# HGRN mixer: half-column level masks, decoded outer products on TensorE, and the next stage's first slabs split one stage earlier

## The reference, cut to what matters

```python
def gla_chunked(q, k, v, log_f, s0):          # chunks of 64 tokens, 4 heads of 128
    ...
        b = jnp.cumsum(gc, axis=1)
        o_inter = jnp.einsum('bthk,bhkv->bthv', qc * jnp.exp(b), s)
        diff = b[:, :, None] - b[:, None, :]
        decay = jnp.where(causal, jnp.exp(jnp.minimum(diff, 0.0)), 0.0)
        att = jnp.einsum('bthk,bshk,btshk->bths', qc, kc, decay)
        o_intra = jnp.einsum('bths,bshv->bthv', att, vc)
        bl = b[:, -1]
        s_new = jnp.exp(bl)[..., None] * s + jnp.einsum('bshk,bshv->bhkv', kc * jnp.exp(bl[:, None] - b), vc)
```

## Time and profile before

| | before |
|---|---|
| median of 3 runs | 2322.16 us (2321.26 to 2322.62) |
| profiled execution, its own time | 2319.34 us |
| its span in the profile | 2317.6 us |
| PE busy | 2205.4 us (95%) |
| DVE busy | 1703.0 us (73%) |
| ACT busy | 1312.3 us (57%) |
| POOL busy | 1005.7 us (43%) |

### The profile page before, as it was taken

One profiled execution on the slowest core, in us unless ns is written; L12 is line 12 of the kernel. 1 busy time (PEld: TensorE's weight loads), 2 busy tenths in 40 slices (PEclk: granted clock), 3 DMA queues, 4 the chain that ended last, 5 costly groups with the idle time before them and its releaser, 6 DMA issues. The chain is left out here.

```text
span 2317.6 us, 46270 instructions
## 1 busy us (share of the span) xinstructions
PE 2205.4 (95%) x15487; PEld 1987.3 (86%) x15487; DVE 1703.0 (73%) x3914; ACT 1312.3 (57%) x3001; POOL 1005.7 (43%) x807
## 2 busy tenths in 40 slices
PE   8889899999999999999989898999999999999998
PEld 8878699999999877888878787999999997788886
DVE  6787379959999656666646555899699995566666
ACT  5434365557777555555546544645577765555554
POOL 6654246997777600000033243389877773000000
PEclk9989899999999999999989999999999999999999
DMA  7728454554444565555544483445444446555553
GB/s 268 126 77 332 185 174 148 170 179 149 155 156 155 199 206 173 185 189 184 187 137 152 144 355 126 164 163 171 163 155 157 154 150 218 191 189 184 189 186 123
DMA packets 115512, 409.33 MB, mean 177 GB/s; under 512 B 20026, under 2 KB 22242, under 8 KB 110050
## 3 DMA queue, kind: packets, MB, share of 16 engines
q1 hardware_dynamic: 111328, 391.45, 50.9%
q0 software_dynamic: 4032, 15.86, 2.1%
HBM read 397.11 MB, written 10.14 MB: 176 GB/s over the span
## 5 line engine op out<-in xcount | busy, mean ns | idle before, releaser
L2011 POOL TENSOR_TENSOR slab_ring_lo<-slab_ring,u_hi 128x512 fp32r<-128x512 f32 x512 | 676.9, 1347 | 182.9 <-ACT u_hi L2107 182.2
L2053 PE MATMUL banks<-operand_hi,u_hi 128*128 128x264 f32 x2048 | 595.7, 291 | 2.7 <-POOL slab_ring_lo L2011 2.7
L2055 PE MATMUL banks<-operand_hi,slab_ring_lo 128*128 128x264 f32 x2048 | 584.9, 286 | 0.0
L2054 PE MATMUL banks<-operand_lo,u_hi 128*128 128x264 f32 x2048 | 584.0, 285 | 0.0
L270 POOL TENSOR_TENSOR slab_ring_lo<-slab_ring,slab_hi 128x512 fp32r<-128x512 f32 x152 | 203.8, 1343 | 667.4 <-ACT slab_hi L260 661.5
L2463 DVE TENSOR_TENSOR operand_lo<-slab_ring,operand_hi 128x512 fp32r<-128x512 f32 x512 | 353.0, 692 | 130.6 <-ACT operand_hi L2428 126.3
L2511 PE MATMUL banks<-operand_hi,w_hi 128*128 128x512 f32 x1024 | 409.7, 400 | 9.9 <-DVE w_lo L2459 9.9
L2512 PE MATMUL banks<-operand_hi,w_lo 128*128 128x512 f32 x1024 | 407.7, 398 | 0.0
L2513 PE MATMUL banks<-operand_lo,w_hi 128*128 128x512 f32 x1024 | 407.6, 398 | 0.0
L2053 PEld LDWEIGHTS banks<-operand_hi,u_hi 128*128 128x128 f32 x2048 | 388.3, 190 | 4.6 <-POOL slab_ring_lo L2011 3.5
L2107 ACT ACTIVATE u_hi<-slab_ring 128x512 fp32r<-128x512 f32 x512 | 322.0, 631 | 122.0 <-PE banks L2055 121.3
(11 more groups left out here) (401 smaller groups left out, 3746.8 us busy)
## 6 DMA issues: line engine op xcount, KB each, us to landing
slab_ring<-in_u SPq DMA_DIRECT2D x256, 512.0 KB, 3.3
slab_ring<-in_v SPq DMA_DIRECT2D x256, 512.0 KB, 4.2
slab_ring<-in_proj SPq DMA_DIRECT2D x144, 512.0 KB, 3.4
cache_k_T<-in_cache_k SPq DMA_DIRECT2D x16, 1024.0 KB, 8.7
cache_v<-in_cache_v SPq DMA_DIRECT2D x16, 1024.0 KB, 13.1
memory_T<-in_mem POOLq DMA_DIRECT2D x2, 1024.0 KB, 5.1
sample_state<-in_state POOLq DMA_DIRECT2D x1, 2048.0 KB, 11.5
out_mem_k_out<-mem_k_T SPq DMA_DIRECT2D x16, 128.0 KB, 2.3
```

Source lines behind the costliest of these rows:

```text
L2011: nc.gpsimd.tensor_tensor(step.ring_lo[:, s, g * HC:(g + 1) * HC, :], step.slab(s)[:, g * HC:(g + 1) * HC, :], hi[:, buf].bitcast(F32), AL ...
L2053: nc.tensor.matmul(bank, hi[:, buf, k, :], xh[:, c, :], start=(c == 0), stop=False)
L2054: nc.tensor.matmul(bank, hi[:, buf, k, :], xl[:, c, :], start=False, stop=False)
L2055: last = nc.tensor.matmul(bank, step.ring_lo[:, s, c, :], xh[:, c, :], start=False, stop=(c == DC - 1))
```

## The change

The gates' iota in PSUM, which the change's name mentions, is in both versions. What differs:

1. `masked`: only the queries of the second run of each pair carry anything new at a level, so mask and add run on half of the 1024 columns, in runs of `half` (every second column at level 0). Level "0" (the identity mask) stays whole.
2. Decoded states: PE transposes the samples' values and keys to rows in `mixer_in` (two transposes after product 18); ACT copies them to SBUF; POOL makes blocks `value row x one-hot sample` on 32 partitions; `outer(k)` on PE multiplies the key rows by such a block, so that four outer products lie in a bank; DVE does `s0 = s0 * fg + bank` in one instruction for each of the four 128-column states. POOL's four decays (L1179) and DVE's L1253, L1258 go.
3. DVE's splits of slabs 6 to 12 move to POOL; POOL also splits slabs 16 and 17, the next block's first two, and ACT rounds them at the end of `mixer_attention`. In layer 1 the same two are split at the end of `window_prompt`. `Fold` with split=2 leaves them out.
4. `difference(2)` and `qe` move from the end of `mixer_in` to the start of `mixer_attention` on DVE, and PE waits for `qe` before the third product.
5. Memory pair 11 moves from before the outputs to after them, 12 from before the norm's means to after.
6. The pooling contexts are gathered by two ACT copies into one tile and stored after the second memory-key store instead of first.

```diff
@@ class Fold
-    def __init__(self, step, layer, which, count, room):
+    def __init__(self, step, layer, which, count, room, split=0):
...
-        split_high(step, act, self.base)
+        if not self.split:
+            split_high(step, act, self.base)
...
         for j in range(DC + self.count):
-            split_low(step, pool, self.base + j, (0,))
+            if j >= self.split:
+                split_low(step, pool, self.base + j, (0,))
...
-    fold = Fold(step, layer, 0, DC, room)
+    fold = Fold(step, layer, 0, DC, room, 2)
@@ mixer_in, PE
+                    if j == 18:
+                        pe.wait_ge(s_cp, H4)
+                        pe.wait_ge(s_kk, 1)
+                        pe.wait_ge(step.constants_ready, 32)
+                        for w, src in enumerate((vi, kk)):
+                            last = nc.tensor.transpose(ps[0:NS, 6, w * P:(w + 1) * P], src[:, NP:NP + NS], step.ident)
+                        last.then_inc(s_rT, 1)
@@ mixer_in, DVE
                     elif n == H4 + 2:
                         difference(dve, 1)
-                        difference(dve, 2)
-                        dve.wait_ge(s_eb, 1)
-                        nc.vector.tensor_tensor(qe[:], qs[:, 0:NP], ecum[:], ALU.mult)
@@ mixer_attention, SP
-                step.store(sp, io["pool_prompt"], u_ext[:, :, TP:TP + CTX])
-                step.store(sp, io["pool_sample"], s_ext[:, :, :, 1:CTX + 1])
                 for k in range(2 * DC):
+                    if k == 2:
+                        sp.wait_ge(s_po, 1)
+                        step.store(sp, io["pool_prompt"], pool_out[:, :, 0, :])
+                        step.store(sp, io["pool_sample"], pool_out[:, :, 1:, :])
@@ mixer_attention, PE
+                def outer(k):
+                    pe.wait_ge(s_row, 1)
+                    pe.wait_ge(s_dg, k // 4 + 1)
+                    if k:
+                        pe.wait_ge(s_kv, k)
+                    nc.tensor.matmul(ps[:, 6, :], rows[:, 1, :], blocks[k // 4][:, 512 * (k % 4):512 * (k % 4 + 1)],
                                      start=True, stop=True).then_inc(s_vb, 1)
...
-                memory_pair(5 + NL)
                 sample_out(6)
...
-                memory_pair(12)
+                memory_pair(11)
                 pool_product(2)
...
+                memory_pair(12)
+                pool_product(3)
                 memory_pair(13)
-                pool_product(3)
@@ mixer_attention, ACT
                 def high_and_copy(k):
-                    if k + 2 < 2 * DC:
-                        split_high(step, act, base + k + 2)
+                    split_high(step, act, base + k + 2)
@@ mixer_attention, POOL (the loop over windows)
                 for g in range(H4):
-                    low(8 + g, (0,))
+                    low(7 + g, (0, 1))
...
-                for k in range(13, 2 * DC):
+                for k in range(7 + H4, 2 * DC + 2):
                     low(k, (0, 1))
@@ mixer_attention, DVE
                 def masked(n, bank, mask):
                     dve.wait_ge(s_pd, n + 1)
...
+                    if n > 1:
+                        dve.wait_ge(s_ad, n - 1)
+                    half = CHUNK if n == 1 else LEVELS[n - 2]
...
+                    view = lambda ap: ap.rearrange("p (s n two t) -> p s n two t", s=NP // P, two=2, t=half)[:, :, :, 1, :]
+                    once = mask.rearrange("p (n two t) -> p n two t", two=2, t=half)[:, :, 1, :]
...
+                        nc.vector.tensor_tensor(view(part), view(two_banks(bank)),
+                                                once.unsqueeze(1).to_broadcast([P, NP // P, P // (2 * half), half]),
+                                                ALU.mult).then_inc(s_mk, 1)
+                    dve.wait_ge(s_mk, n + 1)
+                    nc.vector.tensor_tensor(later(att), later(att), later(part), ALU.add).then_inc(s_ad, 1)
...
                 def sample_state(k):
-                    dve.wait_ge(s_fs, k // 2 + 1)
+                    dve.wait_ge(state_ready, 16)
                     dve.wait_ge(s_vb, k + 1)
-                    outer = diag[k // 4][:, 512 * (k % 4):512 * (k % 4 + 1)].rearrange("p (a b) -> p a b", a=4)
-                    nc.vector.tensor_tensor(outer, ps[:, 6, :].rearrange("p (a b) -> p a b", a=4),
-                                            kk[:, NP + 4 * k:NP + 4 * k + 4].unsqueeze(2).to_broadcast([P, 4, P]),
-                                            ALU.mult).then_inc(s_kv, 1)
-                    dve.wait_ge(s_kv, 2 * k + 1)
-                    st = s0[:, 4 * k:4 * k + 4, :]
-                    nc.vector.tensor_tensor(st, st, outer, ALU.add).then_inc(s_kv, 1)
+                    for c in range(4 * k, 4 * k + 4):
+                        last = nc.vector.scalar_tensor_tensor(out=s0[:, c, :], in0=s0[:, c, :], scalar=fg[:, NP + c:NP + c + 1],
+                                                              in1=ps[:, 6, (c % 4) * P:(c % 4 + 1) * P], op0=ALU.mult, op1=ALU.add)
+                    last.then_inc(s_kv, 1)
...
                 operand(dve, 0)
+                difference(dve, 2)
+                nc.vector.tensor_tensor(qe[:], qs[:, 0:NP], ecum[:], ALU.mult).then_inc(s_qe, 1)
...
                 for i in range(NL):
-                    split_low(step, dve, base + 6 + i, (1,))
                     if i and i + 1 < NL:
                         operand(dve, i + 1)
```

More of the change, by code:

```diff
@@ L306 @@
 class Fold:
-    def __init__(self, step, layer, which, count, room):
-        self.step, self.layer, self.which, self.count = step, layer, which, count
+    def __init__(self, step, layer, which, count, room, split=0):
+        self.step, self.layer, self.which, self.count, self.split = step, layer, which, count, split
         self.base = step.used
@@ L440, in vector @@
                                     ALU.subtract).then_inc(self.mixed_lo, 1)
-            if c == HC - 1:
+            if c == HC - 1 and not self.split:
                 split_low(step, dve, self.base, (1,))
@@ L1435, in _ @@
                 pool.wait_ge(s_k, 1)
-                for k in range(2, 2 * DC):
+                for k in range(2, 2 * DC + 2):
                     split_low(step, pool, base + k, (0,))
-                slabs_split(step, pool, base + 2 * DC - 1)
+                slabs_split(step, pool, base + 2 * DC + 1)
             @block.sync
```

110 lines of the change are left out of this document (53 added, 57 removed).

## The result

| | before | after |
|---|---|---|
| runs beside each other, median | 2321.71 us (4 runs, 2318.59 to 2322.62) | 2298.75 us (4 runs, 2289.42 to 2302.72) |
| ratio, 95% interval | 1 | 0.9906 (0.989 to 0.9923) |
| the same kernel a second time | 2315.49 us (12 runs) | 2296.72 us (6 runs), 0.9921 (0.9905 to 0.9936) |
| profiled execution, its span | 2319.34, 2317.6 us | 2289.42, 2287.7 us |
| from the first level product to the first output product | 60.73 us | 39.87 us |

What follows compares the result with a forecast made beforehand. TensorE was taken to bound nearly everything except layer 0's level stage, which belonged to DVE. Terms from -19.2 for that stage summed to -20.1 us; from the median 2322.16 this gave 2302 us, range 2295 to 2312.

Steps and rivals of the forecast that it cites:

- a ring through DVE's split: Layer 0's level stage: difference, exponentials on ACT, splits on ACT and DVE, operand, mask, add wait in a circle; levels 10.6 us apart.
- The stage, -19.2 to 41.5: First level product to first output product, layer 0: from 60.73 to 41.5 us, bounds -23.7 and -5.2.
- The floor: TensorE's own work in the changed level stage, summed from row prices: 36.9, say 37.0 us.
- the sum for the port, 43.6: Level stage: POOL's 30.9 us and DVE's 12.7 us of two-SBUF-input instructions, run one after the other.
- PE alone: Rival: level stage 37.0 us at full clock and mixer_in at its best, 2295.5 us; chance 0.09.
- POOL: Level stage: POOL busy 30.9 us, main releaser of PE's remaining waits; as the bound, a rival at 2310.5 us, chance 0.22.
- Pair 11, +3.1: Memory pair 11 moves from the level stage to behind it: 2.92 us and its transposes, slower by 3.1.
- Splits ahead of the copies, +1.1: End of mixer_attention: ACT rounds slabs 16 and 17 before copying banks PE waits for, +0.55 us twice.
- mixer_in's end, -1.7: PE's 3.78 us barrier wait for DVE shortens as difference 2 and qe leave; bounds -0.9 and -3.4.
- The clock at the start, -0.7: First key products, at the low level (3.17 against 1.95 us), may escape it after a shorter wait; 0 to -1.7.
- The stores, nothing: Pool stores moved later in SP's queue: slab comes in time, but nothing counted since PE ran through ACT's 7.92 us wait.
- Slower, by short runs: Rival: DVE masks and adds on short column runs cost several times more; at 3 us each, 2330 us; chance 0.03.

Runs made afterwards that it cites:

- 3: Changed kernel with outer products contracted over 128 partitions, ones in place of the decoded states' keys (values differ): 2295.95 us, stage 38.6 us.
- 5: Changed kernel with masks and adds of levels 1 to 6 over all 1024 columns again: 2305.33 us, 0.994 of the kernel before, stage 45.0 us.
- 7: Changed kernel with both pool stores first in SyncE's queue again, reading the strided windows: 2300.64 us, 0.9922 of the kernel before, stage 43.8 us.
- 4: Changed kernel with slabs 16 and 17 split in the next block again, in both layers: 2295.75 us, 0.9917 of the kernel before.
- 6: Changed kernel with difference of pair 2 and decayed queries back in mixer_in on DVE: 2305.0 us, 0.9939 of the kernel before, stage 39.9 us.
- 2: Changed kernel with the second halves of the splits of slabs 6 to 12 back on DVE: 2305.36 us, 0.9957 of the kernel before, stage 49.7 us.
- 12: Changed kernel with tail transposes inside the pair's products and decoded states' rows zero-padded to 128 partitions: 2291.18 us, 0.9898 of the kernel before, stage 38.6 us.

## Why the prediction was right

The time lies in the stated range (2302.0 forecast, 2298.75 and 2296.72 measured), and what the change removes was read rightly: a ring through DVE's split, paid twice through the clock. What bounds the changed stage was not: it is PE's own work, and not the port of DVE and POOL. The likeliest case, 2298 to 2307, holds the first median by 0.75 us and not the second; as a ratio the forecast is 0.9913, between the two measured, 0.9906 and 0.9921. That the total comes so close is partly luck, since errors of opposite sign met: the landmarks up to the first product of out_mixer_0 give -17.7 us and the start of out_mixer_1 -1.4, together -19.1 where -20.1 was summed. Step by step:

- **The stage, -19.2 to 41.5.** Measured -20.9 to 39.9. Two errors met. The floor was mis-sized, since rows were taken from places with other neighbours: 5.9 us a turn has a level at 1.71 and the outer product at 0.86. In the loop the level takes 1.80, and the outer product takes 0.95 even with 128 rows and 0.20 more with 32 (shown in 3). It is not another line's price: the same line takes 1.70 us behind a 128*128 product and 1.80 behind the state read of 128*32 (rows in the last section). 6 x 0.35 = 2.1, so the floor is 39.1, close to PE's busy time of 39.07. And the sum for the port, 43.6, did not bind: the port does stretch DVE's and POOL's rows, but operands made ahead kept PE fed for the six levels. The rival "PE alone" so describes this stage better than the forecast, with the floor 2 us too low. That the port was near is shown by 5 and 7: 1.1 us more of DVE each turn, or one POOL instruction moved into the stage, and 4 to 5 us are lost.
- **POOL.** It was to be busy 30.9 us of the stage and the main releaser of PE's waits. It is busy 36.37: fourteen slab halves fall into the stage and not ten, as POOL runs ahead to slabs 11 and 12 (5.40 us for four halves at 134.14), and what it shares with DVE is stretched. But PE has one wait, of 0.80 us, and that for DVE. DVE's adds, expected at 0.68 us, take 0.93 to 1.34 beside POOL.
- **Pair 11, +3.1.** The tail grew by 4.3 us (23.7 to 28.0), of which 1.0 is the next term.
- **Splits ahead of the copies, +1.1, and out_mixer_0's start, -1.1.** Measured +1.03 and -1.44 (in 4).
- **out_mixer_1, -1.1, and the chunks' way, -0.5.** Measured -1.4 in all from the last store's end.
- **mixer_in's end, -1.7.** The wait went from 3.78 to 1.96, -1.8, and 6 puts it back to 3.60. The start of the block itself moved by 0.3 only (78.15, 77.82), since PE's last product of mixer_in came 1.5 us later in that execution; that is within the scatter of this landmark. Over all fourteen profiles the block starts at 76.8 to 79.4 in the ten with the edit (mean 78.1) and at 78.2 to 81.2 in the four without it (mean 79.7), 1.6 apart where 1.7 was forecast.
- **The clock at the start, -0.7.** The key products took 1.95 instead of 3.17; 6 shows 1.2 us net for the stretch. It does not come each time: in 3 they took 3.02 behind the short wait. The idle time of 2.4 us or more that the prediction read from its rows is no border either, as a level in 5 took 3.48 us behind 2.05 of idle.
- **The stores, nothing.** Wrong: 3.9 us of the stage by 7. I asked only whether PE ran through ACT's wait, and not what POOL, which becomes nearly full in this kernel, would have to do later. The term was hidden in the stage's total.
- **Slower, by short runs.** Refuted: every mask takes 0.68 or 0.69 us, at all run lengths, and the adds take 0.69 us where POOL rests (111.50 in the kernel of 2).

## What to carry to other kernels

Follow a slow turn through all engines until it closes; the instruction that closes it is worth what it waits for besides its own length, and more once its new engine has room (here seven splits of 0.7 us, 4.9 in all: 5.3 us of the stage alone, 9.8 with the other edits). When an engine turns into the bound, price its turn by rows of the same shape that also stand between the same neighbours, or the floor is too low. And an idle time ahead of a stage is not free if the engine that idles will be nearly full inside it.

## What the runs showed of the hardware

- A 512-column product over 32 partitions costs TensorE 0.20 us more a turn than one over 128, in 3 and 12 alike. The weight loads (PEld) in front show where, first in the changed kernel, then in 3:

```profile
110.01 0.28 PE L294 MATMUL banks<-memory_hi,slab_ring_lo 128*128 128x256 f32 x1
110.22 0.29 PEld L1035 LDWEIGHTS banks<-query_T,sample_value_key_rows 32*128 32x128 f32 x2
```

```profile
109.35 0.28 PE L294 MATMUL banks<-memory_hi,slab_ring_lo 128*128 128x256 f32 x1
109.35 0.31 PEld L1035 LDWEIGHTS banks<-query_T,constants 128*128 128x128 f32 x2
```

  The load for 128 rows starts with the product before it and is hidden; the load for 32 rows starts 0.21 us behind that product's start, together with its own. The Trainium skill, page "TensorE: Matmul & The Clock Gate", section "LDWEIGHTS (loading the stationary operand)", says that a 32x128 load takes the same time as a 128x128 one. The trace agrees on the duration (0.29 and 0.31 for two); what differs is that it isn't hidden. Why the engine doesn't hide it no run here shows.
- A product with 32 columns costs too. The first and second level of kernel 12, the same line and operands of the same shape, behind a 128*128 product and behind the state read:

```profile
100.05 1.95 PE L1065 MATMUL banks<-level_operand 128*128 128x128 f32 x16
101.75 0.36 PE L292 MATMUL banks<-memory_hi,slab_hi 128*128 128x256 f32 x1
...
105.62 0.43 PE L1049 MATMUL banks<-sample_state,forget_gate 128*32 128x128 f32 x8
105.98 2.05 PE L1065 MATMUL banks<-level_operand 128*128 128x128 f32 x16
107.78 0.37 PE L292 MATMUL banks<-memory_hi,slab_hi 128*128 128x256 f32 x1
```

  From its start to the next product the first takes 1.70 us and the second 1.80.
- Storing 240 KB in 60-byte pieces took 17.6 us (7), and 4.6 us from a compact tile in the changed kernel; ACT stood 9.7 us for the slab queued behind it.
- The code that all the kernels share scatters by several microseconds from execution to execution: 35.4 to 38.5 in one cross-attention, 800.6 to 804.6 in one PEER stage. A single pair of profiled spans (29.9 us apart) overstated a change of about 20.
